# Seven half-size block products for the output projection of the mixed heads

## The reference

```python
h = rmsnorm(x, norm_mix_w);  proj = h @ w_in            # 1024 x 3600 columns, split over heads
o_gla  = head_rmsnorm(gla_chunked(...))    * silu(gate)  # 4 heads, 512 columns
o_diff = head_rmsnorm(diff_attention(...)) * silu(gate)  # 4 heads, 512 columns
mixed  = concat([o_gla, o_diff])                         # (1024 tokens, 1024)
x = x + mixed @ w_out                                    # the output projection that is changed
x = x + cross_attention(rmsnorm(x), rmsnorm(mem), w_cq, w_ckv, w_co)
return rmsnorm(x, final_norm_w)
```

## Time and profile before

| what | value |
|---|---|
| median of 3 runs | 860.91 us (860.82 to 861.14) |
| the profiled execution's own time | 860.86 us |
| its span, first to last instruction | 859.1 us |
| granted TensorE clock | 1.00 of full speed (2.4 GHz) throughout |
| PE busy | 841.6 us, 98% |
| DVE / ACT / POOL busy | 61% / 46% / 5% |
| HBM traffic | 58.44 MB read, 8.39 MB written |

### The profile page before, as it was taken

How to read it: one execution, slowest core, us unless ns; L and a number is a source line. 1 busy time by engine, 2 the same in 40 slices (tenths; PEclk the granted TensorE clock), 3 DMA queues, 4 the chain that set the end, 5 groups by cost and what they waited for, 6 DMA issues and landing times.

```text
span 859.1 us, 13023 instructions
## 1 busy us (share of the span) xinstructions
PE 841.6 (98%) x4686; PEld 700.9 (82%) x4686; DVE 527.0 (61%) x1273; ACT 398.1 (46%) x982; POOL 46.1 (5%) x87
## 2 busy tenths in 40 slices
PE   8999999999999999999999899999999999999997
PEld 6877888888788888888878798888888888888885
DVE  6667668676678678668768866133346563455543
ACT  7765445444355446345546655103435453225422
POOL 2000000000000000000000000000100000000001
PEclk9999999999999999999999999999999999999999
DMA  8321112112112112112122367431122022251112
GB/s 287 99 79 37 35 40 68 45 43 63 35 35 55 35 32 56 34 32 83 47 68 68 106 200 243 162 108 40 38 86 80 31 83 75 93 180 50 50 49 98
DMA packets 53592, 67.69 MB, mean 79 GB/s; under 512 B 5844, under 2 KB 32536, under 8 KB 53528
## 3 DMA queue, kind: packets, MB, share of 16 engines
q1 hardware_dynamic: 51224, 62.65, 22.9%
q10 hardware_dynamic: 2304, 4.20, 1.5%
HBM read 58.44 MB, written 8.39 MB: 78 GB/s over the span
## 4 chain that ended last, share of the span: by engine, by line
PE 94%; DVE 2%; issue 1%; ACT 1%; DMA 0%; POOL 0%; POOLq 0%; DVEq 0%; ACTq 0%
PE bank L1370 15%; PE bank L1372 15%; PE bank L1371 15%; PE banks2to L1370 9%; PE banks2to L1372 9%; PE banks2to L1371 9%; PE banks6to L1421 5%; PE banks2to L1608 4%; PE bank L1634 3%; PE banks2to L1544 1%; PE bank L1636 1%; PE banks6to L1568 1%; PE banks6to L1372 1%; PE banks6to L1370 1%; PE banks6to L1371 1%
## 5 line engine op out<-in xcount | busy, mean ns | idle before, releaser
L1370 PE MATMUL bank<-w_hi,actT_hi 128*128 128x512 f32 x464 | 186.3, 401 | 0.3
L1372 PE MATMUL bank<-w_hi,actT_lo 128*128 128x512 f32 x464 | 181.4, 391 | 0.0
L1371 PE MATMUL bank<-w_lo,actT_hi 128*128 128x512 f32 x464 | 180.9, 390 | 0.0
L1028 DVE SCALAR_TENSOR_TENSOR w_lo<-w_raw,vecs,w_hi 128x512 fp32r<-128x512 f32 x120 | 86.8, 748 | 43.8 <-ACT w_hi L802 43.7
L1370 PEld LDWEIGHTS bank<-w_hi,actT_hi 128*128 128x128 f32 x464 | 88.0, 190 | 18.7 <-DVE w_lo L1028 1.4
L1372 PEld LDWEIGHTS bank<-w_hi,actT_lo 128*128 128x128 f32 x464 | 87.1, 188 | 18.9
L1371 PEld LDWEIGHTS bank<-w_lo,actT_hi 128*128 128x128 f32 x464 | 87.4, 188 | 16.5
L802 ACT ACTIVATE w_hi<-w_raw,vecs 128x512 fp32r<-128x512 f32 x120 | 82.6, 718 | 12.2 <-DMA w_raw<-in_w_cq 6.4
L1370 PE MATMUL banks2to<-w_hi,actT_hi 128*128 128x512 f32 x176 | 69.7, 396 | 0.0
L1372 PE MATMUL banks2to<-w_hi,actT_lo 128*128 128x512 f32 x176 | 68.7, 390 | 0.0
L1371 PE MATMUL banks2to<-w_lo,actT_hi 128*128 128x512 f32 x176 | 68.6, 390 | 0.0
(11 more groups left out here) (287 smaller groups left out, 1773.5 us busy)
## 6 DMA issues: line engine op xcount, KB each, us to landing
w_raw<-in_w_in SPq DMA_DIRECT2D x56, 256.0 KB, 2.8
w_raw<-in_w_ckv SPq DMA_DIRECT2D x32, 256.0 KB, 3.5
w_raw<-in_w_cq SPq DMA_DIRECT2D x32, 256.0 KB, 2.8
w_raw<-in_w_co SPq DMA_DIRECT2D x32, 256.0 KB, 2.7
stage_in<-in_x SPq DMA_DIRECT2D x8, 512.0 KB, 4.6
tile_a<-mixed ACTq DMA_DIRECT2D x16, 256.0 KB, 3.2
w_raw<-in_w_out SPq DMA_DIRECT2D x16, 256.0 KB, 2.9
x_res<-in_x SPq DMA_DIRECT2D x8, 512.0 KB, 5.2
```

The source lines that it names most:

```text
L1028: return dve.scalar_tensor_tensor(dst, src, scale, hi.bitcast(F32), ALU.mult, ALU.subtract)
L1370: pe.matmul(dst, l_hi, r_hi, start=start, stop=False)
L1371: pe.matmul(dst, l_hi, r_lo, start=False, stop=False)
L1372: return pe.matmul(dst, l_lo, r_hi, start=False, stop=stop)
```

## The change

The product of a 2x2 block matrix by a 2x2 block matrix is formed with 7 block products in place of 8, at the price of sums of blocks. The blocks of the transposed `mixed` are a11 and a12 (tokens 512 to 1023; rows 0 to 511 and 512 to 1023 of the contraction) and a21, a22 (tokens 0 to 511). Those of `w_out` are quarters of 512x512, that is 4 weight tiles each. A product p of tile t, now `X p t` (p = 0 to 6, t = 0 to 3), has 4 contraction tiles of 3 matmuls with 512 columns.

- MT: DVE alone reads the transposed bank and multiplies it by `scale_out` into a float32 tile, `mixT`, that lies in the memory of `actT_hi`. The weights have no scale any more.
- A new stage `xa p t` splits the operand of product p for tile t (128x512): ACT writes hi, DVE lo, from SBUF. There are 28. Those of products 0 and 1 stand between the K and V stages, the others one product ahead (those of products 5 and 6 both in product 4).
- `asum` (10, all on POOL): sums of activation blocks, 128x1024 elements each. `wsum` (16 of 128x512): sums of weight blocks; 8 on POOL (t3 and t2 of tiles 0 and 1, t4 of all four) and 8 on DVE. `cadd` (10 on POOL, 128x1024): adds of the common partial sums to the residual in `x_res`.
- The weight splits of the projection are 28 instead of 16. `w_out` is loaded as 4 raw tiles and 16 tiles in other places (`high_rows`, `low_rows`), through `xw12`, `xw21`, `xw22` on SP.
- A bank of product 0 is copied by ACT into `partial`; those of products 1 to 6 are added by DVE to `partial` or to `x_res`. The bank of product 4 is also copied by ACT. The X stages use six banks.
- HT of the first four tiles moves into product 5, `nsq` into products 4 and 6, the final norm's weight is loaded in product 6.

The diff, cut to what the prediction speaks of:

```diff
+        if n < 4:
+            plan.extend([("xa", 0, n), *([("asum", which, n // 2) for which in ("s3", "s2", "s1")] if n % 2 else [])])
+        else:
+            plan.append(("xa", 1, n - 4))
+        if n >= 6:
+            plan.extend([("xw12", 2 * n - 12), ("xw12", 2 * n - 11)])
+        if n == 6:
+            plan.extend([("wsum", "t3", 0), ("wsum", "t3", 1)])
     assert n_turned == 2 * TT
-    for t in range(TT):
-        plan.extend([("X", 0, t), ("loadx", t + 3) if t + 3 < TT else ("loadw",)][:2 if t < 6 else 1])
-    for t in range(TT):
-        plan.extend([("X", 1, t), ("nsq", t)])
-        if 1 <= t <= 4:
-            plan.extend(("HT", t - 1, kk) for kk in range(2))
+    plan.extend([("wsum", "t2", 0), ("wsum", "t2", 1), ("loadx", 6), ("loadx", 7)])
+    for p in range(7):
+        for t in range(TT // 2):
+            plan.append(("X", p, t))
+            first, second = t % 2 == 0, t % 2 == 1
+            if p == 0:
+                plan.extend([("loadx", t), *([("wsum", "t3", t + 2), ("wsum", "t2", t + 2)] if t < 2 else [])])
+                plan.extend([("wsum", "t1", 2 * t - 4), ("wsum", "t1", 2 * t - 3)] if t >= 2 else [])
+            elif p < 5:
+                plan.append(("xa", p + 1, t))
+            if p == 4:
+                plan.append(("xa", 6, t))
+            if p in (0, 1, 2, 4) and second:
+                plan.append(("cadd", (0, 1, 2, None, 4)[p], t // 2))
+            if p == 1:
+                plan.extend([("xw21", t), ("wsum", "t4", t)])
+            elif p == 2:
+                plan.extend([("xw22", t), *([("asum", "s5", t // 2)] if first else [])])
+            elif p == 3:
+                plan.append(("cadd", 3, t) if t < 2 else ("asum", "s4", t - 2))
+            elif p == 4:
+                plan.append(("nsq", t))
+            elif p == 5:
+                plan.extend([("HT", t, 0), ("HT", t, 1)])
+            elif p == 6:
+                plan.extend([("nsq", TT // 2 + t), *([("loadw",)] if t == 0 else [])])
...
+            if use[g][0][0] == "X":          # where the weight splits of product p stand
+                p = use[g][0][1]
+                if p == 0:
+                    where = ("V", 1, 0) if k < 2 else ("MT", TT - 1, 1)
+                else:
+                    where = ("X", p - 1, (k // 2 + 1) if p == 1 else (k + 1) // 2)
...
+                elif kind == "cadd":         # GpSimd
+                    if which in (0, 4):
+                        pool.wait_ge(pr_copy, t + 2 + which)
+                    elif which in (1, 2):
+                        pool.wait_ge(pr_dve, EVICTED[("X", which, t + 1)])
...
+                    total = x_res[:, row + t:row + t + 2, WC * g:WC * g + WC]
+                    pool.tensor_tensor(total, total, partial(t, 2), ALU.add).then_inc(sum_pool, 1)
...
+                elif kind == "MT":           # VectorE
+                    dve.tensor_scalar(mixT[:, 4 * kk:4 * kk + 4, cols(t)], ps, scale_out[:, kk:kk + 1], None,
+                                      ALU.mult).then_inc(ring_dve, 1)
+                elif kind == "xa":
+                    src, hi, lo = operand(*w)
+                    dve.wait_ge(xa_act, SPLIT_X[stage] + 1)
+                    lo_part(lo, src, hi).then_inc(xa_dve, 1)
...
+                elif kind == "X" and w[0] > 0:
+                    p, t = w
+                    dve.wait_ge(*matmuls_done(stage))
+                    ps = banks[LATE_BANK[stage]]
+                    if p < 6:
+                        sum_ready(dve, ("cadd", p - 1, t // 2))
+                    row, g = ((0, 0), (0, 1), (4, 1), (4, 0))[max(p - 3, 0)]
+                    total = partial(t) if p < 3 else x_res[:, row + t, WC * g:WC * g + WC]
+                    dve.tensor_tensor(total, total, ps, ALU.subtract if p == 3 else ALU.add).then_inc(pr_dve, 1)
...
+                    p, t = w                 # TensorE, stage X
+                    pe.wait_ge(xa_dve, SPLIT_X[("xa", p, t)] + 1)
+                    ps = late_bank(stage)
+                    _, l_hi, l_lo = operand(p, t)
+                    for k in range(KT // 2):
+                        n = W0[X_GROUP + p] + k
+                        if stage in FIRST_USE:
+                            pe.wait_ge(w_dve, n + 1)
+                        last = mm3(ps, l_hi[:, k, :], l_lo[:, k, :], w_hi[:, SLOT[n], :], w_lo[:, SLOT[n], :],
+                                   k == 0, k == KT // 2 - 1)
```

More of the change, by code:

```diff
@@ L72, in group_stages @@
     use += [[("V", g, m) for m in range(MT)] for g in range(2)]
-    use += [[("X", g, t) for t in range(TT)] for g in range(2)]
+    use += [[("X", p, t) for t in range(TT // 2)] for p in range(7)]
     asked = [[[("Q", half, 2 * g + c // 2, c % 2) for c in range(4)] for g in range(2)] for half in range(2)]
@@ L251, in with_weights @@
         early = NW - KT
-        for k in range(KT):
+        for k in range(NK[g]):
+            if use[g][0][0] == "X":
+                p = use[g][0][1]
+                if p == 0:
+                    where = ("V", 1, 0) if k < 2 else ("MT", TT - 1, 1)
+                else:
+                    where = ("X", p - 1, (k // 2 + 1) if p == 1 else (k + 1) // 2)
+                after.setdefault(where, []).append(("w", W0[g] + k))
+                continue
+            if before[0][0] == "X":
+                where = ("X", 5, 3) if k < 2 else ("X", 6, k // 2 - 1)
+                after.setdefault(where, []).append(("w", W0[g] + k))
+                continue
             where = before[(k + 1) * len(before) // (early + 1)] if k < early and len(before) > 4 else (
@@ L258, in with_weights @@
                 where = ("PT", 0, XH - 2, 1)
-            if before[0][0] == "V" and k < 3:
-                where = ("MT", 4 + 2 * before[0][1], 1)
+            if before[0] == ("V", 0, 0) and k < 3:
+                where = ("MT", 4, 1)
             if where == ("proj", GLA_STEPS + DIFF_STEPS - 2):
@@ L304, with sum_counts, on_dve @@
 TR = rings({"T", "MT", "HT", "PT"})
+TURN_ACT = rings({"T", "HT", "PT"})
+SPLIT_X = rings({"xa"})
+def sum_counts():
+    by_pool, by_dve = {}, {}
+    for stage in PLAN:
+        if stage[0] in ("asum", "cadd") or (stage[0] == "wsum" and not on_dve(stage)):
+            by_pool[stage] = len(by_pool) + 1
+        elif stage[0] == "wsum":
+            by_dve[stage] = len(by_dve) + 1
+    return by_pool, by_dve
+def on_dve(stage):
+    return stage[0] == "wsum" and (stage[1] == "t1" or (stage[1] in ("t3", "t2") and stage[2] >= 2))
+POOL_SUM, DVE_SUM = sum_counts()
 def ring_bank(stage):
@@ L328, in late_banks @@
         bank[("K", c)] = b
+    for p in range(7):
+        for t in range(TT // 2):
+            bank[("X", p, t)] = (*PJ_BANKS, 4, 5)[(4 * p + t) % 6]
     a, b, c, d = (PJ_BANKS[(PJ[("Q", 1, XH - 1, 0)] + n) % 4] for n in range(4))
@@ L356, in own_signals, with evictions @@
     return out
+def evictions():
+    count, out = 0, {}
+    for stage in PJ:
+        count += stage[:2] != ("X", 0)
+        out[stage] = count
+    return out
+EVICTED = evictions()
 PROJ_DONE = own_signals({"proj"})
@@ new lines, in sum_ready, with add_rows @@
+        def sum_ready(eng, stage):
+            if on_dve(stage):
+                eng.wait_ge(sum_dve, DVE_SUM[stage])
+            else:
+                eng.wait_ge(sum_pool, POOL_SUM[stage])
+        def add_rows(eng, which, k):
+            raw = w_raw[:, k, :]
+            if which == "t3":
+                return eng.tensor_tensor(high_rows[k], high_rows[k], low_rows[k], ALU.subtract)
+            if which == "t2":
+                return eng.tensor_tensor(sum_rows[k], high_rows[k], raw, ALU.add)
+            if which == "t1":
+                return eng.tensor_tensor(raw, low_rows[k], raw, ALU.subtract)
+            return eng.tensor_tensor(sum_rows[k], sum_rows[k], low_rows[k], ALU.subtract)
```

289 lines of the change are left out of this document (234 added, 55 removed).

## The result

| kernel | median us | ratio to before (95% interval) |
|---|---|---|
| before | 860.88 (4 runs) | |
| after the change | 878.53 (876.78 to 879.1, 4 runs) | 1.0201 (1.0186 to 1.0215) |

The change costs 17.7 us; the forecast was 8.3 us less than before. The time lies outside the range of 849.4 to 869. The profiled execution, the fastest of the four (876.78 us), has a span of 875.0 us against 859.1, 15.9 more. All of that arises before the queries: the first matmul of Q starts at 638.6 us instead of 622.67. The projection itself starts at 538.92 us instead of 531.99. So K and V cost 6.9 us more, and the projection 9.0 us more, where 10.9 us less were due.

The account below looks back on a forecast made before the run. PE, busy 98%, was taken to bound the kernel. Matmuls -10.88 and K/V waits +2.2 gave -8.7 us from 860.86, 852.2; with 0.05 for the median and 0.4 for the switch to Q, 852.6 (own range 850.4 to 857; outer 849.4 to 869).

Parts of the forecast that it names:

- The matmuls: Projection: 336 matmuls instead of 384, 48 fewer at 0.2267 us each, 10.88 us less.
- GpSimd's own time: GpSimd's block sums: 2.3 us for 1024 columns, 1.15 for 512, so it would keep up in the products.
- The other reading, 7.0 us: GpSimd at 7.0 us for 128x1024, earlier instructions read as they stand; as a rival about 925 us, chance 0.02.
- DVE by itself: Projection: DVE's own work is 7.2 us in products 0 to 3, 9.6 in 4 and 5, all below 10.88.
- shared fairly by need it just fits: 0 us: Products 0 to 4: GpSimd and DVE excluding each other exceed the time by 11.2 us, slack covers it, no cost.
- slack of 11.6: Products: 4.8 us at the cadd plus 6.8 from DVE writing operands 3 stages before PE wants them.
- K and V: K and V stages: operand splits behind a GpSimd instruction stall PE 1.0 and 1.2 us, 2.2 us taken.
- The bound of 5 us: K and V stages: upper limit of the stall, a wait of 2.3 us at two splits each.
- The second rival: K, V and products: strict turns, two-input DVE instructions wait for whole GpSimd ones; 871 us, from 857 to 873, chance 0.33.
- DVE's instructions come in bursts: Argument against strict turns: DVE works in bursts of 2 to 4 between waits for PE; no size given.
- the split at 13.15 us: Earlier trace: DVE split began 0.18 us before a small GpSimd instruction ended, took its usual 0.75 us; cited for no exclusion.
- The rule: SBUF port pair: GpSimd and two-input DVE instructions lock it for a whole instruction, whichever starts first, and block the other.

Follow-up runs that it names:

- e1: Changed kernel with each GpSimd block sum replaced by two memsets of its destination, which read nothing (sums wrong): 850.86 us, ratio 0.9883.
- e2: Changed kernel with GpSimd's in-place sums cut to one column and its others made memsets (sums wrong), hardly any GpSimd work: 850.57 us.
- e3: Changed kernel with each GpSimd sum issued as two instructions of half the columns, same bytes: 866.94 us, ratio 1.0069.
- e9: Fastest version with all sums on DVE and its work spread, but the ten cadd adds put back on GpSimd: 861.41 us, ratio 1.0006.
- e5: Changed kernel with only the six activation sums between the K and V stages moved from GpSimd to DVE: 873.27 us.
- e6: Changed kernel with 72 idle PE transposes, 8 ahead of each of certain weight waits in products 2 to 4: 877.74 us, ratio 1.0197.

## Why the prediction was wrong

- **The matmuls, right.** -10.88 us; e1 and e2 measured -10.1 and -10.4 with the work of DVE, ACT and the transfers in place.
- **GpSimd's own time, right for the large sums, with some luck.** 2.3 us were taken for 128x1024, from two waits seen in the earlier trace rows; a sum that met no split before it took 2.40 us. For 512 columns 1.15 were taken, and 1.30 measured, 13% more. The reading left out a fixed part: e3's sums of 256 columns took 0.74 us, and with 1.30 and 2.40 that makes about 0.28 us per 128 columns and 0.2 us on top (estimated from these three). The 0.29 us read for a whole instruction of 128 columns was therefore too little for it and happened to be right as a slope. The other reading, 7.0 us, is out. The estimate of 2.25 us from the Trainium skill's page "GPSIMD Engine Reference" is 6% below the row.
- **DVE by itself, right.** e1: 7.6 us a product against 7.2 worked out.
- **The step that failed** is "shared fairly by need it just fits: 0 us". It added the times of both engines (65.6 us in 54.4) and set them against a slack of 11.6 as if a split had to wait only when the sum of all work demanded it. With the measured 2.40 and 1.30 us the same sum is 67.8, 13.4 too much, and would still leave only 1.8 us; PE waited 12.3 us in the products, HT included. What the runs show in its place is turns that don't ask for need: while GpSimd has something ready, the next split stands behind a whole sum, 2.9 us for 0.6 us of work. GpSimd does its sums early, and the splits that PE wants come late. With four sums a product DVE needs 7.2 + 4 x 2.3 = 16.4 us where it has 10.9 (an estimate from the rows above); from 565 to 599 us its 28 instructions, 17 us of work, took 34. e3 shows that the length of a turn decides, e9 that it hurts without a backlog.
- **K and V, mis-sized.** 2.2 us were taken, PE waited 4.8 (2.0 and 2.9), and the projection starts 6.9 us later; the low clock behind the first wait is 1.8 of that. e5, in which 2.2 us of waits are left, is 5.3 us faster, more than the waits that went, so here the clock did cost time. The bound of 5 us was right for the waits, without the clock.
- **The second rival was what happened**, with its mechanism and place: waits for weight splits in products 2 to 4, 3.3, 3.0 and 3.9 us, where 3.0, 6.1 and 6.9 were worked out. It gave 871, 7.5 us short. With HT the waits behind K and V were 12.3 us and not 16; the low clock and what is unassigned, 9.6 us, stood in no case, and part of it takes the place of waits (e6). It had 0.33. It was weighed down by "DVE's instructions come in bursts" and by the split at 13.15 us in the earlier trace rows. That one met only the last 0.18 us of a GpSimd instruction of one element per partition and could say nothing on a long read.
- **The rule.** "SBUF — State Buffer", section "SBUF: two separate sides", of the Trainium skill speaks of a lock for a whole instruction. This trace agrees, with 2.87 us for a split of 0.68, and e1 agrees with its restriction to GpSimd instructions that read. The prediction quoted the rule and then summed as if the port went to whoever needed it more.

What stays open: why PE's clock fell after some waits and not after others of the same length (2.0 us at 514 yes, 2.9 us at 531 no), the 1.7 us that the accounts leave, and the one add in e9 that waited for four instructions of DVE.

## What to carry to other kernels

Before work goes to an idle GpSimd, count the DVE instructions with two SBUF operands beside it. Charge one of them for each GpSimd instruction with that one's whole length: here an add of 2.4 us on GpSimd cost DVE 1.6 to 2.2 us of waiting, more than the 1.14 us of doing it itself. An idle share of 95% says nothing on that. With these sums on GpSimd the kernel became 17.7 us slower, with all of them on the busier DVE 2.8 and, spread out, 7.9 us faster. Where GpSimd must share, short instructions, or ones that only write, do least harm. A lower clock is no cost where the engine only comes earlier to its next wait, as from 565 to 599 us here; where others wait for it, as behind 599, it is one.

## What the runs showed of the hardware that was not expected

- A blocked instruction counts as busy: GpSimd's sums are shown with 2.82 us when splits stood between them and 2.40 when none did, DVE's splits with 2.87 and 0.68. DVE at "100%" from 565 to 599 us did 28 instructions of 0.6 us, half of what its busy time says.
- GpSimd's memset of 128x1024 float32 took 0.955 us beside two-operand instructions of DVE, and slowed none of them: e1's splits of these tiles took 0.68 to 0.69 us.
- PE's granted clock fell to 0.50 for 2 to 5 us after some waits of 2 to 3 us. With 8 transposes ahead of each awaited matmul of products 2 to 4 (e6) it stayed at 1.00 there, though waits of up to 2.1 us were left.
